# Matmuls of ones at the start, two earlier weight loads and a chunk-by-chunk second pair of tiles in a gated convolution and retention layer

## The chip, the cores and the metric

The kernel runs on one core of one Trainium2 chip. The metric is the device time in microseconds of one execution. The kernel before was timed three times, and its median is 1497.3 us.

## What is computed

One decoder layer over T = 1032 token columns, 1024 of a new sequence and 8 single tokens of other sequences. Cut to the part that the change touches, the reference is

```python
proj = rms_norm(x, n_mix_pre) @ w_in          # T x 1024 times 1024 x 7168
a_val, a_gate, q, k, v, g, gate_a, gate_b = split(proj)
u = a_val * sigmoid(a_gate)                   # T x 512, input of the 31-tap convolution
conv = depthwise_conv(concat(history, u)) + b_dw
```

Behind it come layer norm and SiLU of `conv`, the chunkwise retention of q, k and v, the gated merge with two output projections, and a squared-ReLU MLP of width 4096, with an RMS norm ahead of and behind both halves. Everything is 32-bit floating point.

## The kernel before, in words

Activations lie transposed: 128 channels on the partitions, T columns along them, and 8 such tiles `k` for the 1024 channels. The columns are cut in 3 chunks `c` of 344. Weights come in slots of four 128x128 tiles (256 KB), so that one output tile of 128 channels needs two slots, called its halves here (k 0 to 3 and k 4 to 7). Most products are made of three fast matmuls: an operand is split into a rounded high part (made by ScalarE, written ACT in the profile) and the rest as a low part, and high x high, high x low and low x high are summed in PSUM (`PARTS`, `tile_mms`, line 1026).

The kernel is raw: every engine has its own list of instructions in a fixed order, with semaphores between them. An instruction whose semaphore is not there blocks all behind it on its engine.

Output tiles are called groups g. Six PSUM banks form two sets of three, one bank for each chunk, and the groups take the sets in turn. The first groups make the four pairs (gate tile, value tile) of `u`:

- Pair 0 (`G_U`, `G_U + 1`) is made by `plain_mms` (line 1064) as full 32-bit matmuls from the raw `x_in` and weights `wp` with the norm gain multiplied in, before the norm of x is known. Slot `wp[:, 0]` is scaled by VectorE (DVE, line 2286), slots 1 to 3 by GpSimd (POOL, line 862). The order on TensorE (PE) is, for chunk 0: gate tile half 0 from `wp` 0, value tile half 0 from `wp` 1, gate half 1 from `wp` 2, value half 1 from `wp` 3. Chunks 1 and 2 go tile by tile. One column sum `x_stat` (line 1062) of each chunk feeds the root of the norm (`x_rms`, ACT lines 1527 and 1529), which writes `rr`. DVE then multiplies the six banks by `rr` (`u_factor`, line 2280), ACT makes the sigmoid of the gate tile (`u_gate(0)`, line 1576, which waits for five of the six `u_factor`), and DVE multiplies by it (`u_out(0)`, line 2355).
- Meanwhile `x_in` is normalised: `x_scale` (DVE 2264), `x_hi` (ACT 1557, high parts `xn_h`), `x_lo` (DVE 2272, low parts `xn_l`), each by chunk and half.
- Pair 1 (`G_U + 2`, `G_U + 3`) is made by `second_mms` (line 1078) from weight slots 4 to 7: first the gate tile over all three chunks, then the value tile over all three. A tile's two halves each raise the semaphore `mm` when they are done for the last chunk.
- Pairs 2 and 3 are made by `group8` (line 1031) from slots 8 to 15, one slot after the other, each over all three chunks.

The high parts of slots 8 and on are made on ACT by `weight_hi(n)` (line 1566); for n = 8 and 9 it waits until the slot n - 4 has been used for the last time, for those behind until the slot n - 2 has. On ACT it stands between other work:

```python
act.wait_ge(xn_lo, CHUNKS * KT)
for k in range(KT):
    x_gain(k)                 # L1580
    if k == 0:
        weight_hi(8)
    if k == 2:
        u_gate(1)
        weight_hi(9)
```

`u_gate(1)` waits until the gate tile of pair 1 is complete. The low parts are made on POOL by `low_part` (line 870). POOL makes the low part of slot 8, then waits for all eight `x_gain` (`pool.wait_ge(xs_sc, KT)`), then makes two sums `x_sum` (line 885), and then the low part of slot 9; from there one `x_sum` (lines 885 to 894) and one `low_part` take turns.

Of the kernel before, what the change touches and what calls it, by code (L numbers as in the profile page):

```python
# [24 lines left out]
ALU = mybir.AluOpType  # L25
ACT = mybir.ActivationFunctionType

P = 128
# [3 lines left out]
T = SEQ + DEC  # L32
CHUNKS = 3
# [5 lines left out]
HIST = TAPS - 1  # L39
# [34 lines left out]
G_U, S_U = 1, 0  # L74
# [40 lines left out]
LN_ADD, LN_SQUARE = {13: 1, 15: 2, 17: 3}, {10: (0, 1), 14: (2,), 16: (3,)}  # L115
ORDER = (0, 1, 3, 2, 5, 4, 6)
NSLOT = 264


def build(nc, xT, wseq, vecs, wdwT, cacheT, s_in, rope, mask_d, ident_d,  # L120
# [8 lines left out]
    with ExitStack() as ctx:  # L129
# [19 lines left out]
        u_ext, a_C1 = place("u_ext", [P, CT, UW])  # L149
        q0s, _ = place("q0s", [P, 2, T], F32, a_C1 + 4 * 2128)  # L150
# [4 lines left out]
        raw, _ = place("raw", [P, RAW, SLOT])  # L155
        w_h, _ = place("w_h", [P, HL, SLOT], F32R)
        w_l, _ = place("w_l", [P, HL, SLOT], F32R)
# [3 lines left out]
        sx_h, _ = place("sx_h", [P, 3, QK, HT], F32R, a_B)  # L161
        sx_l2, _ = place("sx_l2", [P, QK, HT], F32R, a_B + 12 * QK * HT)
        sx_l, _ = place("sx_l", [P, 2, QK, HT], F32R, a_A)
        sx_5, _ = place("sx_5", [P, QK, HT], F32, a_G + 4 * QK * HT)
        wx_h, _ = place("wx_h", [P, SLOT], F32R, a_C0)
        wx_l, _ = place("wx_l", [P, SLOT], F32R, a_C0 + 4 * SLOT)
        wx_x, _ = place("wx_x", [P, SLOT], F32, a_C0 + 8 * SLOT)
        wx_y, _ = place("wx_y", [P, SLOT], F32, a_C0 + 12 * SLOT)
        gst, _ = place("gst", [P, 8, HT], F32, a_G)
        gst_c, _ = place("gst_c", [P, 8, HT], F32, a_C1)  # L170
        sgm, _ = place("sgm", [P, 8, HT], F32, a_Y)
        silu, _ = place("silu", [P, T], F32, a_Q)
        cvq_h, _ = place("cvq_h", [P, T], F32R, a_Q)
        cva_h, _ = place("cva_h", [P, CT, T], F32R, a_B)
        cva_l, _ = place("cva_l", [P, CT, T], F32R, a_A)
        gt0, _ = place("gt0", [P, 4, T], F32, a_D)
        gt1, _ = place("gt1", [P, 4, T], F32, a_B + 16 * T)
        gb, _ = place("gb", [P, KT, T], F32, a_D)
        bop_b, _ = place("bop_b", [P, 4, T], F32, a_B)
        bop_a, _ = place("bop_a", [P, 2, T], F32, a_A + 8 * T)  # L180
        ma, _ = place("ma", [P, KT, T], F32, a_E)

        mg_h, _ = place("mg_h", [P, KT, T], F32R, a_A)
        mg_l, _ = place("mg_l", [P, KT, T], F32R, a_B)
        fx_h, _ = place("fx_h", [P, KT, T], F32R, a_A)
        fx_l, _ = place("fx_l", [P, KT, T], F32R, a_B)

        stg_a, _ = place("stg_a", [P, KT, T], F32, a_A)
        stg_b, _ = place("stg_b", [P, KT, T], F32, a_B)

        wp, _ = place("wp", [P, RAW, SLOT], F32, a_C2)
        wc_h, _ = place("wc_h", [P, 2, SLOT], F32R, a_C2 + 8 * T)
        wc_l, _ = place("wc_l", [P, 2, SLOT], F32R, a_C2 + 8 * T + 8 * SLOT)
        rr, _ = place("rr", [P, T], F32, a_G + 4 * T)
        cv_l, _ = place("cv_l", [P, CT, T], F32R, a_C2)
        qk1, _ = place("qk1", [P, 4, T], F32, a_C2)
        v1, _ = place("v1", [P, 4, T], F32, a_C1)
        ro1_h, _ = place("ro1_h", [P, 4, T], F32R, a_C2)
        ro1_l, _ = place("ro1_l", [P, 4, T], F32R, a_C1)
        h_res, _ = place("h_res", [P, KT, T], F32, a_C1)  # L200
        fac, _ = place("fac", [P, KT, T], F32, a_C0)
        op0, _ = place("op0", [P, QK, HT], F32, a_C0)
        hq_c, _ = place("hq_c", [P, 4, HT], F32, a_C0 + 8 * T)
        hq_d, _ = place("hq_d", [P, 8, HT], F32, a_C0 + 16 * T)
        hq_e, _ = place("hq_e", [P, 4, HT], F32, a_C0 + 32 * T)

        qk0, _ = place("qk0", [P, 4, T], F32, a_G)
        v0, _ = place("v0", [P, 4, T], F32, a_Y)
        ro0_h, _ = place("ro0_h", [P, 4, T], F32R, a_G)
        ro0_l, _ = place("ro0_l", [P, 4, T], F32R, a_Y)  # L210
        mix, _ = place("mix", [P, KT, T], F32, a_D)
        tx_l, _ = place("tx_l", [P, KT, T], F32R, a_D)

        wo_h, _ = place("wo_h", [P, 8, SLOT], F32R, a_E)
        wo_l, _ = place("wo_l", [P, 8, SLOT], F32R, a_E + 32 * SLOT)
        tx_h, _ = place("tx_h", [P, KT, T], F32R, a_E)

        sgt, _ = place("sgt", [P, T], F32, a_G)
        hist, _ = place("hist", [P, CT, DEC, TAPS], F32, a_Q)
        hprod, _ = place("hprod", [P, DEC, TAPS], F32, a_Q + 4 * CT * DEC * TAPS)  # L220
        hq_g, _ = place("hq_g", [P, 8, HT], F32, a_G)

        mask, _ = place("mask", [P, RC])
# [32 lines left out]
        def pset(g, n=CH):  # L256

            return ps[:, 3 * (g % 2):3 * (g % 2) + 3, 0:n]
# [4 lines left out]
        def t3(ap):  # L263

            return ap.rearrange("p (c n) -> p c n", c=CHUNKS)
# [142 lines left out]
        def done(slot):  # L408

            return slot + 1 + HL  # L410
# [163 lines left out]
        def taken(e, g, shift=0):  # L574


            e.wait_ge(ps_free[g % 2], shift + (g // 2 + 1))

        def free_set(pe, g, shift=0):

            if g >= 2:
                taken(pe, g - 2, shift)
# [15 lines left out]

        @block.sync
        def _(sp):  # L600
            sp.dma_start(x_in[:, 0:2, 0:CH], xT[:, 0:2, 0:CH]).then_inc(xa_in[0], 16)
            sp.dma_start(wp[:, 0, :], wseq[0]).then_inc(gate_ld[0], 16)
            sp.dma_start(x_in[:, 4:6, 0:CH], xT[:, 4:6, 0:CH]).then_inc(xa_in[2], 16)
            for s, n in ((1, 2), (2, 1), (3, 3)):
                sp.dma_start(wp[:, s, :], wseq[n]).then_inc(gate_ld[s], 16)
            for i in range(2):
                sp.dma_start(x_in[:, 4 * i:4 * i + 4, CH:2 * CH], xT[:, 4 * i:4 * i + 4, CH:2 * CH]
# [407 lines left out]
        def _(pe):  # L1015
# [48 lines left out]
            def plain_mms(c, t, half):  # L1064

                if c == 0 and half + t:
                    pe.wait_ge(w_split, 2 * half + t + 1)
                for sub in range(SLOT_TILES):
                    k = SLOT_TILES * half + sub
                    if (c, t) == (0, 0) and k in (0, 2):  # L1070
                        pe.wait_ge(w0_sc, k // 2 + 1)
                    if c == 0 and k % 2 == 0:
                        pe.wait_ge(xa_in[k // 2], 16)
                    out = pe.matmul(pch(G_U + t, c), wp[:, 2 * half + t, sub * P:(sub + 1) * P],  # L1074
                                    x_in[:, k, c * CH:(c + 1) * CH], start=(k == 0), stop=(k == KT - 1))
                return out

            def second_mms(t, c, half):
# [10 lines left out]
                                   (wc_h, wc_l) if t else W)  # L1089
                return out  # L1090

            plain_mms(0, 0, 0)
            plain_mms(0, 1, 0)
            plain_mms(0, 0, 1).then_inc(u_mm, 1)
# [13 lines left out]
            plain_mms(2, 1, 0)  # L1108
            plain_mms(2, 1, 1).then_inc(u_mm, 1)
            pe.sem_inc(mm, RAW)  # L1110
            for t in range(2):
                free_set(pe, G_U + 2 + t)
                for c in range(CHUNKS):
                    for half in range(2):
                        out = second_mms(t, c, half)
                        if c == CHUNKS - 1:
                            out.then_inc(mm, 1)
# [1102 lines left out]
        def _(dve):  # L2220
# [37 lines left out]
            def x_scale(c, half):  # L2258

                xs = x_in[:, 4 * half:4 * half + 4, c * CH:(c + 1) * CH]  # L2260
                if half == 0:
                    dve.wait_ge(rms_rs, R_X + c + 1)
                    dve.wait_ge(u_mm, 2 * c + 2)
                dve.tensor_tensor(xs, xs, rr[:, c * CH:(c + 1) * CH].unsqueeze(1).broadcast_to([P, 4, CH]), ALU.mult
                                  ).then_inc(x_sc, 1)
# [9 lines left out]
            def u_factor(c, t):  # L2275

                dve.wait_ge(rms_rs, R_X + c + 1)
                dve.wait_ge(u_mm, 2 * c + t + 1)
                rows = pch(G_U + t, c)
                dve.tensor_tensor(rows, rows, rr[:, c * CH:(c + 1) * CH], ALU.mult).then_inc(u_rr, 1)  # L2280

            dve.wait_ge(cst_ld, 16)
            dve.wait_ge(gate_ld[0], 16)
            for k in (0, 2):
# [12 lines left out]
            x_scale(1, 0)  # L2297
            u_factor(1, 0)
            u_factor(1, 1)
            x_scale(1, 1)  # L2300
            u_factor(2, 0)
            x_lo(1, 0)
            x_scale(2, 0)
            x_lo(1, 1)
            x_scale(2, 1)
            x_lo(2, 0)
            u_factor(2, 1)
            x_lo(2, 1)


# [34 lines left out]
            dve.wait_ge(wdw_ld, 48)  # L2345
            dve.wait_ge(hist_ld, 16)

            def u_out(j):

                g = G_U + 1 + 2 * j  # L2350
                if j == 0:
                    dve.wait_ge(u_rr, 2 * CHUNKS)
                dve.wait_ge(mm, done(S_U + 4 * j + 3))
                taken(dve, g - 1)
                dve.tensor_tensor(t3(u_ext[:, j, HIST:HIST + T]), pset(g), t3(sgt[:]), ALU.mult
                                  ).then_inc(ps_free[g % 2], 1)
                taken(dve, g)

            def u_sample(j):

                dve.tensor_copy(hist[:, j, :, HIST], u_ext[:, j, HIST + SEQ:HIST + T]).then_inc(h_done, 1)
# [17 lines left out]
                dve.tensor_tensor(sx_l2[:] if i == 2 else sx_l[:, i - 3], src, sx_h[:, i - 2].bitcast(F32),  # L2379
                                  ALU.subtract).then_inc(xs_lo, 1)  # L2380

            u_out(0)
            u_sample(0)
            taps(10)
            u_out(1)
# [768 lines left out]
```

## Time and profile before

| | |
|---|---|
| median of 3 runs | 1497.3 us |
| the 3 runs | 1497.29, 1497.96, 1497.30 us |
| span of the profiled execution | 1495.6 us |
| the profiled execution's own time | not recorded; the median is 1.7 us above the span |
| PE matmul busy | 1475.2 us, 99% |
| PE weight load busy | 1455.2 us, 97% |
| DVE, ACT, POOL busy | 1001.0, 635.4, 842.0 us |

The span runs from the first to the last instruction of the execution that the profiler took. Times in rows are microseconds from its start. "PE" is the matmul part of TensorE, "PEld" its weight loads. In a timeline a row is a run of like instructions: start, length, engine, line, operation, tiles, shape, count, and in brackets the idle time of the engine just ahead and what ended it. A 32-bit matmul shows as two records, the split kind as one.

### The profile page before, as it was taken

Reading aid. Unit: us, or ns where it says so; the run is one execution under the profiler, and the core shown is the slowest. Engines: PE = TensorE matmul, PEld = TensorE weight load, DVE = VectorE, ACT = ScalarE, POOL = GpSimd, SP = SyncE. Lnnn points to the kernel's source line nnn. Section 1 sums busy time; section 2 is a strip of 40 time slices with the busy share of each in tenths; the row PEclk is TensorE's granted clock in tenths of the full one; section 3 lists DMA queues with packets and bytes.
Section 4 is the critical chain, followed back from the end, with each engine's and each line's share of the span. In section 5 each row is a group of like instructions: output and inputs, shape, how many; then the busy total and the mean of one; then the engine's idle time right before and its main releaser. Section 6 shows DMA issues by size and latency. Waiting matters only on the chain.

```text
span 1495.6 us, 28307 instructions
## 1 busy us (share of the span) xinstructions
PE 1475.2 (99%) x11336; PEld 1455.2 (97%) x11336; DVE 1001.0 (67%) x1251; ACT 635.4 (42%) x929; POOL 842.0 (56%) x571
## 2 busy tenths in 40 slices
PE   8999999999999999999999999999999999999996
PEld 5999999999999999999999999999999999999995
DVE  7999888856545724576715876766657765574847
ACT  5533444344544541131213855556556332332333
POOL 3377776777545653257565445555555655554555
PEclk9999999999999999999999999999999999999998
DMA  6013333322356258621421144566759575454634
GB/s 217 22 42 94 114 114 113 113 80 65 112 176 205 75 200 296 219 80 50 149 78 50 29 149 171 199 237 219 253 193 326 203 285 189 142 208 156 227 107 170
DMA packets 110091, 229.13 MB, mean 153 GB/s; under 512 B 8960, under 2 KB 20992, under 8 KB 108304
## 3 DMA queue, kind: packets, MB, share of 16 engines
q1 hardware_dynamic: 95296, 204.30, 39.7%
q10 hardware_dynamic: 14672, 23.09, 4.6%
q8 instruction: 89, 1.46, 0.4%
q14 instruction: 34, 0.28, 0.1%
HBM read 154.41 MB, written 72.95 MB: 152 GB/s over the span
## 4 chain that ended last, share of the span: by engine, by line
PE 96%; POOL 1%; DMA 1%; ACT 1%; issue 1%; DVE 0%; POOLq 0%; SPq 0%; DVEq 0%; ACTq 0%
PE ps L1476 40%; PE ps L1237 26%; PE ps L1026 16%; PE ps L1402 3%; PE ps L1389 3%; PE ps L1074 2%; PE ps L1164 1%; PE ps L1169 1%; PE ps L1180 1%; PE ps L1166 1%; DMA cva_h<-conv_scratch 1%; PE ps L1147 0%; PE ps L1152 0%; PE ps L1194 0%; POOL w_l L931 0%
## 5 line engine op out<-in xcount | busy, mean ns | idle before, releaser
L1476 PE MATMUL ps<-tx_h,w_h 128*128 128x258 f32 x960 | 271.5, 283 | 0.0
L1476 PE MATMUL ps<-tx_l,w_h 128*128 128x258 f32 x960 | 271.3, 283 | 0.0
L1476 PE MATMUL ps<-tx_h,w_l 128*128 128x258 f32 x960 | 271.1, 282 | 0.0
L996 POOL TENSOR_TENSOR w_l<-raw,w_h 128x512 fp32r<-128x512 f32 x120 | 185.6, 1551 | 147.6 <-ACT w_h L2033 147.1
L1476 PE MATMUL ps<-fx_l,w_h 128*128 128x258 f32 x720 | 203.7, 283 | 0.0
L1476 PE MATMUL ps<-fx_h,w_h 128*128 128x258 f32 x720 | 203.6, 283 | 0.0
L1476 PE MATMUL ps<-fx_h,w_l 128*128 128x258 f32 x720 | 203.4, 282 | 0.0
L1476 PEld LDWEIGHTS ps<-tx_h,w_h 128*128 128x128 f32 x960 | 181.4, 189 | 0.1
L1476 PEld LDWEIGHTS ps<-tx_l,w_h 128*128 128x128 f32 x960 | 181.4, 189 | 0.1
L1476 PEld LDWEIGHTS ps<-tx_h,w_l 128*128 128x128 f32 x960 | 181.2, 189 | 0.0
L2328 DVE SCALAR_TENSOR_TENSOR ps<-u_ext,wdw,ps 128x512 f32<-128x512 f32 x232 | 155.2, 749 | 0.0
L2033 ACT ACTIVATE w_h<-raw 128x512 fp32r<-128x512 f32 x120 | 75.7, 631 | 186.8 <-PE ps L1476 179.7
L996 POOL TENSOR_TENSOR w_l<-sum_y,w_h 128x512 fp32r<-128x512 f32 x60 | 91.9, 1532 | 110.2 <-ACT w_h L2033 110.2
L1476 PEld LDWEIGHTS ps<-fx_h,w_h 128*128 128x128 f32 x720 | 136.2, 189 | 0.0
L1476 PEld LDWEIGHTS ps<-fx_l,w_h 128*128 128x128 f32 x720 | 136.0, 189 | 0.0
L1476 PEld LDWEIGHTS ps<-fx_h,w_l 128*128 128x128 f32 x720 | 135.9, 189 | 0.0
L1237 PE MATMUL ps<-xn_h,w_h 128*128 128x258 f32 x416 | 119.6, 287 | 0.0
L1237 PE MATMUL ps<-xn_l,w_h 128*128 128x258 f32 x416 | 117.5, 282 | 0.0
L1237 PE MATMUL ps<-xn_h,w_l 128*128 128x258 f32 x416 | 117.4, 282 | 0.0
L2884 DVE TENSOR_TENSOR fac<-ps,fac 128x516 f32<-128x516 f32 x79 | 54.6, 691 | 83.3 <-PE ps L1476 83.3
L931 POOL TENSOR_TENSOR w_l<-raw,w_h 128x512 fp32r<-128x512 f32 x54 | 76.6, 1418 | 55.2 <-ACT w_h L1650 55.1
L850 POOL TENSOR_TENSOR w_h<-raw,zero 128x512 fp32r<-128x512 f32 x36 | 42.0, 1167 | 108.8 <-PE ps L1026 50.2
(386 smaller groups left out, 4305.4 us busy)
## 6 DMA issues: line engine op xcount, KB each, us to landing
raw<-wseq_dram SPq DMA_DIRECT2D x260, 256.0 KB, 3.1
quad_scratch<-quad_h SPq DMA_DIRECT2D x16, 774.0 KB, 3.5
tx_h<-quad_scratch SPq DMA_DIRECT2D x12, 1032.0 KB, 10.4
tx_l<-hidden_scratch SPq DMA_DIRECT2D x12, 1032.0 KB, 12.8
gate_scratch<-gst SPq DMA_DIRECT2D x10, 1032.0 KB, 5.0
hidden_scratch<-hq_g SPq DMA_DIRECT2D x8, 1032.0 KB, 7.0
hidden_scratch<-stg_b SPq DMA_DIRECT2D x6, 1032.0 KB, 6.9
hq_g<-hidden_scratch SPq DMA_DIRECT2D x6, 1032.0 KB, 13.1
```

Source lines behind the costliest of these rows:

```text
L850: pool.tensor_tensor(hi, raw[:, s, :], zero[:, 0:1].broadcast_to([P, SLOT]), ALU.add).then_inc(w_hi, 1)
L931: pool.tensor_tensor(lo, src, hi.bitcast(F32), ALU.subtract).then_inc(xw_lo, 1)
L996: pool.tensor_tensor(lo, src, hi.bitcast(F32), ALU.subtract).then_inc(q_lo, 1)
L1026: out = pe.matmul(pch(g, c), w[a][:, place_, sub * P:(sub + 1) * P], xs[b][:, k, c * CH:(c + 1) * CH], start=(first and n == 0), stop=(las ...
L1074: out = pe.matmul(pch(G_U + t, c), wp[:, 2 * half + t, sub * P:(sub + 1) * P], x_in[:, k, c * CH:(c + 1) * CH], start=(k == 0), stop=(k == ...
L1237: out = pe.matmul(ps[:, 2 * n + s, 0:HC], XRINGS[q % RING][wa][:, kk * P:(kk + 1) * P], x_operand(i, xb, kk, s), start=(i < 3 and kk == 0 ...
L1389: out = pe.matmul(pch(g, m), (wo_h, wo_l)[a][:, slot, sub * P:(sub + 1) * P], MG[b][:, k, c * CH:(c + 1) * CH], start=(k == 0 and n == 0), ...
L1402: out = pe.matmul(pch(g, c), DIRECT_W[slot][a][:, (k % SLOT_TILES) * P:(k % SLOT_TILES + 1) * P], FX[b][:, k, c * CH:(c + 1) * CH], start= ...
L1476: out = pe.matmul(ps[:, 2 * n + s, 0:HC], RINGS[q % RING][wa][:, kk * P:(kk + 1) * P], OPS[x][xb][:, QK * kh + kk, at_:at_ + HC], start=(i ...
L2033: act.activation(RINGS[q % RING][0], src, ACT.Copy).then_inc(q_hi, 1)
L2328: out = dve.scalar_tensor_tensor(dst, u_, w_, bank, ALU.mult, ALU.add)
L2884: dve.tensor_tensor(dst, pair(n), dst, ALU.add).then_inc(ev_d, 1)
```

## The change

Four things are changed:

- Ahead of the first product PE issues nine matmuls of a 128x128 tile of ones by itself into PSUM bank 6, whose content is not used.
- On the queue of SyncE (SP) the load of `wp` 0 goes ahead of that of the first two tiles of x, and the load of `wp` 1 goes ahead of x tiles 4 and 5 instead of behind them.
- Pair 1 goes chunk by chunk: for each chunk first the gate tile and then the value tile.
- On DVE `u_factor(2, 0)` goes ahead of `x_scale(1, 1)`, and `u_factor(2, 1)` and `u_out(0)` go behind it, ahead of `x_lo(1, 0)`. `u_out(0)` stood behind the last `x_lo` before.

The lists of ACT and POOL are the same.

```diff
+WARM = 9
...
         def _(sp):
+            sp.dma_start(wp[:, 0, :], wseq[0]).then_inc(gate_ld[0], 16)
             sp.dma_start(x_in[:, 0:2, 0:CH], xT[:, 0:2, 0:CH]).then_inc(xa_in[0], 16)
-            sp.dma_start(wp[:, 0, :], wseq[0]).then_inc(gate_ld[0], 16)
+            sp.dma_start(wp[:, 1, :], wseq[2]).then_inc(gate_ld[1], 16)
             sp.dma_start(x_in[:, 4:6, 0:CH], xT[:, 4:6, 0:CH]).then_inc(xa_in[2], 16)
-            for s, n in ((1, 2), (2, 1), (3, 3)):
+            for s, n in ((2, 1), (3, 3)):
...
+            for _ in range(WARM):
+                pe.matmul(B6[:, 0:P], ones[:], ones[:], start=True, stop=True)
             plain_mms(0, 0, 0)
...
-            for t in range(2):
-                free_set(pe, G_U + 2 + t)
-                for c in range(CHUNKS):
+            for c in range(CHUNKS):
+                for t in range(2):
+                    if c == 0:
+                        free_set(pe, G_U + 2 + t)
                     for half in range(2):
                         out = second_mms(t, c, half)
                         if c == CHUNKS - 1:
...
             u_factor(1, 0)
             u_factor(1, 1)
+            u_factor(2, 0)
             x_scale(1, 1)
-            u_factor(2, 0)
+            u_factor(2, 1)
+            u_out(0)
             x_lo(1, 0)
             x_scale(2, 0)
             x_lo(1, 1)
             x_scale(2, 1)
             x_lo(2, 0)
-            u_factor(2, 1)
             x_lo(2, 1)
...
-            u_out(0)
             u_sample(0)
             taps(10)
```

## Rows read from the trace of the kernel before

**Rows 1.** The page: busy time of each engine over the span.
```profile
PE 1475.2 (99%) x11336; PEld 1455.2 (97%) x11336; DVE 1001.0 (67%) x1251; ACT 635.4 (42%) x929; POOL 842.0 (56%) x571
```

**Rows 2.** Waits of PE over the whole span (total, times, longest).
```profile
PE ps L1074 <- DVE wp L2286: 5.8, 1, 5.8
PE ps L1237 <- ACT v L1853: 0.2, 1, 0.2
```

**Rows 3.** Timeline of PE.
```profile
5.78 12.39 PE L1074 MATMUL ps<-x_in,wp 128*128 128x344 f32 x32 [5.78 <-DVE wp L2286]
...
31.31 7.10 PE L1074 MATMUL ps<-x_in,wp 128*128 128x344 f32 x24
38.21 0.42 PE L1026 MATMUL ps<-xn_h,w_h 128*128 128x344 f32 x1
...
66.64 0.64 PE L1026 MATMUL ps<-xn_h,w_h 128*128 128x344 f32 x3
```

**Rows 4.** Timeline of the weight loads, 3 to 19 us.
```profile
11.07 0.34 PEld L1074 LDWEIGHTS ps<-x_in,wp 128*128 128x128 f32 x1 [0.24 <-issue]
11.65 5.98 PEld L1074 LDWEIGHTS ps<-x_in,wp 128*128 128x128 f32 x21 [0.24 <-issue]
```

**Rows 5.** Windows: stretch, length, busy time by engine, PEclk (granted clock), DMA share, GB/s.
```profile
6.00:8.00 2.00, 2.00 (x4) 1.26 (x5) 0.89 (x2) 1.14 (x2) 0.00 (x0) 1.00 1.08 388
...
1486.00:1488.00 2.00, 0.00 (x0) 0.00 (x0) 2.00 (x5) 0.00 (x0) 2.00 (x2) 0.55 0.82 309
```

**Rows 6.** Timeline of PE: 128-column matmuls of retention, and the last matmuls.
```profile
383.15 1.05 PE L1164 MATMUL ps<-p_b,vt_b 128*128 128x128 f32 x8
...
1478.63 2.78 PE L1498 MATMUL ps<-hq_g,ones 128*128 128x258 f32 x12
```

**Rows 7.** Timeline of DVE, 16 to 50 us.
```profile
19.90 5.13 DVE L2264 TENSOR_TENSOR x_in<-x_in,rr 128x1376 f32<-128x1376 f32 x2
...
32.73 1.58 DVE L2264 TENSOR_TENSOR x_in<-x_in,rr 128x1376 f32<-128x1376 f32 x1
34.23 0.94 DVE L2280 TENSOR_TENSOR ps<-ps,rr 128x344 f32<-128x344 f32 x2
35.07 1.58 DVE L2264 TENSOR_TENSOR x_in<-x_in,rr 128x1376 f32<-128x1376 f32 x1
36.57 0.52 DVE L2280 TENSOR_TENSOR ps<-ps,rr 128x344 f32<-128x344 f32 x1
37.00 2.03 DVE L2272 SCALAR_TENSOR_TENSOR xn_l<-x_in,vec,xn_h 128x344 fp32r<-128x344 f32 x4
...
48.23 1.23 DVE L2355 TENSOR_TENSOR u_ext<-ps,sgt 128x1032 f32<-128x1032 f32 x1
```

**Rows 8.** Timeline of ACT, 31 to 70 us.
```profile
34.34 2.00 ACT L1557 ACTIVATE xn_h<-x_in,vec 128x344 fp32r<-128x344 f32 x4 [0.52 <-DVE x_in L2264]
37.13 1.03 ACT L1576 ACTIVATE sgt<-ps 128x1032 f32<-128x1032 f32 x1 [0.78 <-DVE ps L2280]
...
48.35 1.16 ACT L1580 ACTIVATE x_in<-x_in,vec 128x1032 f32<-128x1032 f32 x1 [2.32 <-DVE xn_l L2272]
49.41 0.61 ACT L1566 ACTIVATE w_h<-raw 128x512 fp32r<-128x512 f32 x1
...
53.46 5.33 ACT L1580 ACTIVATE x_in<-x_in,vec 128x1032 f32<-128x1032 f32 x5
66.90 0.63 ACT L1566 ACTIVATE w_h<-raw 128x512 fp32r<-128x512 f32 x1 [8.11 <-PE ps L1026]
```

**Rows 9.** Timeline of POOL.
```profile
8.63 4.30 POOL L862 TENSOR_TENSOR wp<-wp,vec 128x512 f32<-128x512 f32 x3 [7.80 <-DMA wp<-wseq_dram]
...
58.87 4.77 POOL L885 TENSOR_TENSOR sx<-x_in 128x1032 f32<-128x1032 f32 x2 [7.47 <-ACT x_in L1580]
63.60 1.29 POOL L870 TENSOR_TENSOR w_l<-raw,w_h 128x512 fp32r<-128x512 f32 x1
```

More of the change, by code:

```diff
@@ L2280, in u_factor, with u_out @@
                 dve.tensor_tensor(rows, rows, rr[:, c * CH:(c + 1) * CH], ALU.mult).then_inc(u_rr, 1)
+            def u_out(j):
+                g = G_U + 1 + 2 * j
+                if j == 0:
+                    dve.wait_ge(u_rr, 2 * CHUNKS)
+                dve.wait_ge(mm, done(S_U + 4 * j + 3))
+                taken(dve, g - 1)
+                dve.tensor_tensor(t3(u_ext[:, j, HIST:HIST + T]), pset(g), t3(sgt[:]), ALU.mult
+                                  ).then_inc(ps_free[g % 2], 1)
+                taken(dve, g)
             dve.wait_ge(cst_ld, 16)
@@ L2346, in _ @@
             dve.wait_ge(hist_ld, 16)
[L2348 to L2357, printed above, removed]
             def u_sample(j):
```

## The prediction

> **What bounds the kernel now.** I read the page's busy times first, then the waits of PE, then the timelines of the four engines over the first 110 us, because all edits lie there. PE is busy 99% of the span [rows 1]. It waits 5.8 us for its first operands and otherwise never over 0.2 us [rows 2]. So PE is the bound from 5.78 us on: what an edit does to its time is what it adds or takes in the instants at which PE may go on, and any new idle time of PE, wherever it lies, ends up in the total almost whole. Whoever reads this should look for two numbers: when the split products start (38.21 us, [rows 3]) and when the second slot of the third pair, slot 9, starts (66.64 us, [rows 3]).
>
> The first part runs slowly. A weight load followed the last every 0.57 us or so up to 11.65 us (11.07 to 11.65), then 21 in 5.98 us, 0.285 each [rows 4]. That is a factor of two, the ratio of the two levels of TensorE's clock, 1.2 and 2.4 GHz. The granted clock reads 1.00 there all the same [rows 5]; the pace is the better witness. About 5.9 us of PE's time were at the low level, so a warm start would shorten PE's own list by up to 2.9 us.
>
> **The change, part by part.**
>
> *Nine matmuls of ones.* Eight records of 128 columns took 1.05 us warm, which holds a drain, so some 0.11 to 0.13 us each [rows 6]; nine 32-bit matmuls are 18 records, at half pace some 4.0 to 4.7 us. Starting at about 1 us, they end between 5 and 5.8, in time that is idle now. I take nothing for them. If they started late they could hold up the first product by up to 1 us; the next paragraphs show that PE has that much room.
>
> *Loads.* `wp` 0 goes out one issue (0.5 us) sooner and `wp` 1 jumps over one load. The first scaling on POOL starts at 8.63 us, and three take 4.30 us [rows 9]; it may start 0.5 to 0.9 us sooner. The four eight-record pieces of chunk 0 take 2.29 us each at full pace. With PE at full pace from about 5.3 us, the first ends at 7.6 us and PE then waits for `wp` 1, scaled at about 9.3 us. Chunk 0 ends at 9.3 + 3 x 2.29 = 16.2 us instead of 18.0, and the whole plain part, whose end by its last row is 31.31 + 7.10 = 38.4 us with its drain [rows 3], some 1.8 us sooner: the next product could start at 36.4 us. So of 2.9 us of clock some 1.1 go to the wait for `wp` 1.
>
> *What that is worth.* The split products need the PSUM set that `u_gate(0)` frees. It ran from 37.13 to 38.16, having waited for `u_factor(2, 0)` (36.57 to 37.09), and PE went on at 38.21 [rows 3, 7, 8]. DVE works without a gap from 19.90 to there [rows 7]; it is held by its own list and by data from memory, not by PE. So PE's gain stops at this gate. The gate moves by the other edit: `u_factor(2, 0)` now starts at about 35.1 and ends at 35.65, and `u_gate(0)` can go as soon as ACT ends `x_hi(1, 0)`, which is held by DVE's `x_scale(1, 0)` and ends at 36.34 [rows 8]. It then runs from 36.25 to 37.3, and the split products start at 37.35: **0.86 us gained**, bounds 0 (a gate as late as before) and 1.8 (PE's own pace).
>
> Here a rule weighs against the row. The Trainium skill (TensorE: Matmul & The Clock Gate, "The HAM clock gate") says that the throttled clock is the default and that activity releases it, so that early matmuls run at half rate. By that alone the ones would bring the whole 2.9 us. The rows agree on the pace and deny the worth, since the engine behind is the one that frees the banks.
>
> *DVE's new order.* Between `x_scale(1, 1)` and `x_lo(1, 0)` now come 0.43 us of `u_factor(2, 1)` and 1.23 us of `u_out(0)`, so that the last `x_lo` ends at about 49.8 instead of 48.3 us [rows 7]. PE reads chunk 1 from 44.9 and chunk 2 from 52.4 us in the new order (24 matmuls of 0.158 us for each tile and chunk: 28.43 us for 180 of them, [rows 3]), and no low part is late. `u_out(0)` ends at 38.9, well ahead of 41.1 us, when the value tile wants its set. Nothing lost, nothing gained here; a wait is bounded by 0 on both sides.
>
> *Chunk by chunk.* This part hurts. Before, the gate tile of pair 1 was finished after 72 matmuls, about 49.6 us. Now it is finished after 120, and its first half after 108. ACT does `x_gain(0)` and then `weight_hi(8)`, which waits for that first half. Before there was no wait: it ran at 49.41 [rows 8]. Now it can run at 37.35 + 107 x 0.158 + 0.32 + 0.11 = 54.7 us (0.32 the length of the last matmul, 0.11 from its end to ACT, as at 66.90, [rows 8]). Behind it in ACT's list are seven `x_gain`, `u_gate(1)` and `weight_hi(9)`, which took from 49.41 to 58.79 = 9.38 us [rows 8]; `u_gate(1)` itself has no further wait (56.2 against 57.3). So the last `x_gain` ends at 64.1 us, 5.3 later. POOL waits for all eight before its two sums: 58.87 becomes 64.15. The low part of slot 9, 63.60 + 1.29 = 64.89 before, follows 6.0 us behind their start [rows 9], so it is there at **70.15 us**. PE wants it after 180 matmuls, at 37.35 + 28.4 = 65.8 us. It had 1.7 us to spare and now waits 4.4 us. Slot 9 starts at 70.2 instead of 66.64: **+3.55 us**, the 0.86 included.
>
> In one line: slot 9's start less before = (split start) + 32.85 - 66.64. Start 37.35 gives +3.55; 36.4 gives +2.6; 38.2 gives +4.4.
>
> *Behind that.* Does it get worse, or is it caught up? POOL goes on with a sum (2.4 us) and slot 10's low part at about 73.6, wanted at 75.9; slot 11 about 79.8, wanted at 81.5; then each slot's high part waits for PE itself again, as before. DVE is 0.3 us late only and starts to wait for PE at its third `u_out`. So everything locks on to PE, 3.55 us late, and since PE has no idle time left to the end, nothing is returned. Sum against the profiled span: 1495.6 + 3.55 = 1499.15; the median stands 1.7 us above that span, so 1500.9 us.
>
> **The rivals.**
>
> *The clock falls in the wait.* After the last matmuls (end 1481.4, [rows 6]) the clock is at 1.00 until just past 1486 and then at half (0.55 over 1486 to 1488, [rows 5]): some 4.8 us of idleness. The new wait is 4.4 us, close to that. If it falls near the wait's end, PE goes at half pace for up to the 5.9 us that the first rise took, and loses up to 2.9 us: 1500.9 to 1503.8, say 1503. Against it: 4.4 is below 4.8, and the only case seen is one. The same page of the Trainium skill says that the gate's point of switching depends on where the activity falls against a free-running counter, so the same program may fall in one run and not in another. Chance 0.18.
>
> *PE's pace carries the head.* If DVE and ACT also come sooner (less waiting for the first sums), the split products start at 36.4 and the loss is +2.6 us, 1499.9. Against: DVE has no gap between 19.90 and 37 [rows 7]. With it go smaller stalls than I count. Chance 0.14.
>
> *The late slot is hidden.* The change is not slower if slot 9's low part is there when PE comes, so that the 0.86 us are kept: 1496.4 us. The place is POOL's wait for the eight `x_gain`. It decides where that end passes 64.1 - 4.4 = 59.7 us, 0.9 us later than before. It would need ACT to reach `weight_hi(8)` by 50.3 us, when the gate tile's last chunk has not begun. Chance 0.04.
>
> *The whole of the cold start comes back.* PE's 2.9 us, with no gate at 37.3, no wait for `wp` 1 and no late slot: 1494.4 us. Three of the steps above would have to be wrong together. Chance 0.01. The skill's rule on the gate, taken alone, gives this.
>
> *The edits at the head do nothing.* Start 38.2, +4.4 us, 1501.7: part of my own range.
>
> **How the numbers follow.** My case (+2.8 to +4.4) has 0.63, the fallen clock 0.18, the faster head 0.14, the hidden slot and the whole cold start 0.05 together. The range runs from 1499.4 to 1503.8: it holds my case, the clock and most of the faster head. A difference of 0.2% is 3.0 us, about what a measurement can tell from none. Slower by over that: the clock and most of my case, 0.74; within: the faster head and the lower edge of my case, 0.22; faster by over it would need 3 us where the gate allows 1.8 at most, 0.04.
>
> **What would show it.** In the profile after: plain weight loads at 0.285 us before 8 us; `u_factor(2, 0)` ahead of 36 us; the split products from about 37.3; ACT idle some 3.5 us ahead of `weight_hi(8)` at 54.7; POOL's two sums from 64.1; one PE wait of about 4.4 us for POOL's low part (line 870), ending at 70.2, and hardly any other but that for `wp` 1. I am wrong if no such wait is there, or if PE waits again at slots 10 or 11, or if the matmuls behind the wait run at half pace.

## The result and the profile after

The changed kernel takes 1502.98 us (median of 5 runs, 1502.14 to 1503.62) against 1497.32 us before (5 runs). The ratio is 1.0037, with a 95% interval of [1.0026, 1.0047]: 5.7 us slower. The forecast was 1500.9 us in a range of 1499.4 to 1503.8, with 1503 as the time of the rival in which the clock falls. The profiled execution is the 1502.98 us one, its span 1500.9 us (most line numbers are higher by 2 to 6 than before). Of all runs told of below one, of the kernel without ones, fell in a slow state of the chip (2419.41 us at a mean granted clock of 0.556) and is left out of the figures.

The page's busy row and PE's waits, which answer to [rows 1, 2]:

```profile
PE 1479.5 (99%) x11354; PEld 1459.9 (97%) x11354; DVE 1001.9 (67%) x1251; ACT 635.5 (42%) x929; POOL 843.0 (56%) x571
```
```profile
PE ps L1028 <- POOL w_l L872: 4.4, 1, 4.4
PE ps L1028 <- ACT sgt L1581: 1.1, 1, 1.1
PE ps L1095 <- DVE eps_b L2236: 1.1, 1, 1.1
```

One new wait for POOL's low part (line 872) stands out, 4.4 us. A second, 1.1 us for the first sigmoid, is the measure of how far PE now runs ahead of that gate. PE's timeline (start, length, line, tiles, count), for [rows 3]:

```profile
5.41 10.40 PE L1076 MATMUL ps<-x_in,wp 128*128 128x344 f32 x32
...
28.94 7.10 PE L1076 MATMUL ps<-x_in,wp 128*128 128x344 f32 x24
37.16 0.43 PE L1028 MATMUL ps<-xn_h,w_h 128*128 128x344 f32 x1 [1.12 <-ACT sgt L1581]
...
65.14 0.62 PE L1028 MATMUL ps<-xn_h,w_l 128*128 128x344 f32 x3
70.13 1.23 PE L1028 MATMUL ps<-xn_h,w_h 128*128 128x344 f32 x3 [4.37 <-POOL w_l L872]
71.16 1.06 PE L1028 MATMUL ps<-xn_l,w_h 128*128 128x344 f32 x3
...
74.60 0.76 PE L1028 MATMUL ps<-xn_h,w_l 128*128 128x344 f32 x3
75.20 0.62 PE L1028 MATMUL ps<-xn_h,w_h 128*128 128x344 f32 x3
```

Slot 9 starts at 70.13, 3.49 us later than before. Behind it PE goes at little over half its pace until 75.20. The windows of that stretch (PE busy and count first, granted clock third from the end) say why:

```profile
66.00:68.00 2.00, 0.00 (x0) 0.00 (x0) 1.97 (x2) 0.49 (x1) 2.00 (x2) 1.00 0.00 0
68.00:70.00 2.00, 0.00 (x0) 0.00 (x0) 1.93 (x3) 0.00 (x0) 2.00 (x2) 0.51 0.00 0
70.00:72.00 2.00, 1.87 (x6) 1.87 (x7) 2.00 (x5) 0.00 (x0) 2.00 (x2) 0.50 0.37 114
72.00:74.00 2.00, 2.00 (x8) 2.00 (x8) 2.00 (x5) 0.00 (x0) 2.00 (x3) 0.50 0.08 26
74.00:76.00 2.00, 2.00 (x12) 2.00 (x12) 2.00 (x5) 0.00 (x0) 2.00 (x1) 0.79 0.43 131
```

The clock fell to half about 68 us, some 2.3 us into the wait, and came back near 74.8. From 71.16 to 74.60 there are four steps from trio to trio (a trio is one row of three matmuls, one for each chunk), 0.86 us each, where full pace has 0.47. Of the 4.7 us that PE worked at half pace, 4.7 x (1 - 0.47 / 0.86) = 2.1 us are lost. With the 3.49 us of lateness that makes 5.6; the measured difference is 5.7 between the medians and 5.3 between the two profiled spans.

The chain that makes slot 9 late, in the timelines of ACT, POOL and DVE ([rows 7 to 9]):

```profile
36.10 1.01 ACT L1581 ACTIVATE sgt<-ps 128x1032 f32<-128x1032 f32 x1
...
49.60 1.16 ACT L1585 ACTIVATE x_in<-x_in,vec 128x1032 f32<-128x1032 f32 x1 [1.90 <-DVE xn_l L2277]
54.50 0.63 ACT L1571 ACTIVATE w_h<-raw 128x512 fp32r<-128x512 f32 x1 [3.75 <-PE ps L1028]
...
58.56 5.33 ACT L1585 ACTIVATE x_in<-x_in,vec 128x1032 f32<-128x1032 f32 x5
```
```profile
63.97 4.71 POOL L887 TENSOR_TENSOR sx<-x_in 128x1032 f32<-128x1032 f32 x2 [7.46 <-ACT x_in L1585]
68.65 1.43 POOL L872 TENSOR_TENSOR w_l<-raw,w_h 128x512 fp32r<-128x512 f32 x1
```
```profile
34.08 1.36 DVE L2285 TENSOR_TENSOR ps<-ps,rr 128x344 f32<-128x344 f32 x3
35.35 1.58 DVE L2269 TENSOR_TENSOR x_in<-x_in,rr 128x1376 f32<-128x1376 f32 x1
```

ACT stands for 3.75 us ahead of slot 8's high part, which now waits for PE; everything behind it on ACT's list, the last five `x_gain` included, is that much later; POOL's two sums start at 63.97 instead of 58.87; slot 9's low part comes at 70.08.

### The profile page after: what moved, and what is told of

The parts are those of the page before. It is cut to its first block, busy times and chain, and to the rows that moved or that the text cites. A ratio compares the mean times of both kernels' runs of the same rounds, so it can differ in the third digit from the quotient of the medians.

```text
span 1500.9 us, 28344 instructions
## 1 busy us (share of the span) xinstructions
PE 1479.5 (99%) x11354; PEld 1459.9 (97%) x11354; DVE 1001.9 (67%) x1251; ACT 635.5 (42%) x929; POOL 843.0 (56%) x571
## 4 chain that ended last, share of the span: by engine, by line
PE 94%; POOL 2%; DVE 2%; ACT 1%; issue 1%; DMA 1%; SPq 0%; POOLq 0%; DVEq 0%; ACTq 0%
PE ps L1481 40%; PE ps L1242 26%; PE ps L1028 15%; PE ps L1407 3%; PE ps L1394 3%; PE ps L1169 1%; PE ps L1174 1%; PE ps L1185 1%; PE ps L1171 1%; DMA x_in<-xT_dram 1%; PE ps L1152 0%; PE ps L1157 0%; PE ps L1199 0%; DVE x_in L2269 0%; ACT x_in L1585 0%
## 5 line engine op out<-in xcount | busy, mean ns | idle before, releaser
L933 POOL TENSOR_TENSOR w_l<-raw,w_h 128x512 fp32r<-128x512 f32 x54 | 76.7, 1421 | 54.7 <-ACT w_h L1655 54.6
```

What stands on the lines that cost most here:

```text
L933: pool.tensor_tensor(lo, src, hi.bitcast(F32), ALU.subtract).then_inc(xw_lo, 1)
```

## The experiments

All run beside the kernel before; its median was 1497.66 us for the first four, 1497.62 for the next four and 1497.48 for the last. Theory at the start: the late slot 9 costs 3.5 us, and the clock that falls in its wait costs 2 more.

### The low part of slot 9 ahead of the sums

```diff
                 low_part(n % RAW, n)
-                if n == 2 * RAW:
+                if n == 2 * RAW + 1:
                     pool.wait_ge(xs_sc, KT)
                     x_sum(0)
-                if 2 * RAW <= n < 15:
+                    x_sum(1)
+                if 2 * RAW < n < 15:
                     x_sum(n - 2 * RAW + 1)
```

> The changed kernel with one move on GpSimd: the low part of slot 9 goes ahead of the wait for the eight x_gain and of the two sums, which then stand behind it with the third. My theory (the late slot 9 costs 3.5 us and the clock that falls in its 4.4 us of waiting some 2 more): slot 9's low part is there at about 60 us, PE does not wait for it and the clock stays up. Left are small waits because the sums still start at 64.0: slot 10 at 72.4 instead of 71.3 (1.1 us), slot 11 some 0.5 more; split products from 37.2. So 1497.3 - 1.05 + 1.6 = 1497.9 us. Rival (the loss lies in pair 1 going chunk by chunk, or in VectorE's new order, by contention or late banks, and the wait for slot 9 is only where it shows): the time stays over 1500.

Measured: 1497.59 us, ratio 1.0000 [0.9991, 1.001] to the kernel before. POOL's timeline and PE's waits:

```profile
58.62 1.29 POOL L872 TENSOR_TENSOR w_l<-raw,w_h 128x512 fp32r<-128x512 f32 x1 [2.23 <-ACT w_h L1572]
```
```profile
PE ps L1029 <- POOL w_l L872: 1.4, 2, 1.1
```

Slot 9's low part is there at 59.9 us, PE's 4.4 us wait is gone, 1.1 us is left for slot 10, and the clock reads 1.00 in every window from 66 to 78. Moving one operation on an engine that the change did not touch takes back the whole loss: the split products start at 37.06, 1.15 us sooner than before, and the small waits for low parts (1.4 us together) take that up. So going chunk by chunk has no further cost that shows here.

### The wait filled with matmuls of ones

```diff
+            def filler(k):
+                if k == SLOT_TILES - 1:
+                    free_set(pe, G_U + 5)
+                    for _ in range(16):
+                        pe.matmul(pch(G_U + 5, 0)[:, 0:P], ones[:], ones[:], start=True, stop=True)
...
+            group8(G_U + 4, S_U + 8, XN, 0, 0, filler)
```

> The changed kernel with 16 matmuls of the tile of ones between slot 8 and slot 9, into a bank that is free and is overwritten later (the loop of the last two pairs is written out for it). They take some 3.7 us of the 4.4 us wait, and the slot arrives as late as before. My theory: PE goes on at 70.1 us as in the changed kernel, but at full pace, so that only the late slot is paid: 1497.3 + 3.5 = 1500.8 us, granted clock 1.00 from 66 to 76 us. Rival (what is lost behind 70 us is not the clock but late weights or contention of the engines): 1503.0 as the changed kernel, or more.

Measured: 1500.79 us, ratio 1.0021 [1.0011, 1.0031]. PE's timeline and the windows:

```profile
65.36 3.73 PE L1128 MATMUL ps<-ones 128*128 128x128 f32 x32
69.91 0.75 PE L1029 MATMUL ps<-xn_h,w_h 128*128 128x344 f32 x3 [0.82 <-POOL w_l L873]
70.49 0.63 PE L1029 MATMUL ps<-xn_l,w_h 128*128 128x344 f32 x3
```
```profile
68.00:70.00 2.00, 1.18 (x11) 0.99 (x10) 1.93 (x4) 0.00 (x0) 2.00 (x3) 1.00 0.00 0
70.00:72.00 2.00, 2.00 (x13) 2.00 (x14) 2.00 (x4) 0.00 (x0) 2.00 (x1) 1.00 0.33 121
```

Slot 9 is as late as in the changed kernel (69.91), but PE goes on at full pace. 1502.98 - 1500.79 = 2.2 us is the clock's part, 1500.79 - 1497.66 = 3.1 us that of the lateness. This splits the loss. The changed kernel was timed at another time, beside a kernel before of 1497.32 and not 1497.66; with each taken against its own, the clock's part is 2.5 us.

### No matmuls of ones

> The changed kernel without the nine matmuls of ones. My theory (the split products wait for the sigmoid of the first gate tile, whose chain does not hang on PE's pace): the plain weight loads go at 0.57 us until 8 to 12 us, the plain products end up to 1.5 us later, which the 1.1 us wait for the sigmoid mostly takes in: the same as the changed kernel within 0.4 us, 1503.0. Rival (the cold clock costs what PE's list says): 1.5 to 2.9 us slower, 1504.5 to 1505.9.

Its edit takes the two lines of the loop over `WARM` out. Measured: 1502.57 us (1502.37 to 1503.05), ratio 1.0033 [1.0019, 1.0046]: no slower than the changed kernel. The weight loads, and the first split product:

```profile
8.16 0.34 PEld L1076 LDWEIGHTS ps<-x_in,wp 128*128 128x128 f32 x1 [0.24 <-issue]
8.73 7.57 PEld L1076 LDWEIGHTS ps<-x_in,wp 128*128 128x128 f32 x26 [0.24 <-issue]
```
```profile
37.39 0.42 PE L1028 MATMUL ps<-xn_h,w_h 128*128 128x344 f32 x1 [0.30 <-ACT sgt L1579]
```

The loads are at half pace until 8.73 us; the split products still wait for the sigmoid, 0.3 us instead of 1.1, and start at 37.39. That is 0.23 us later than with the ones, since the gate takes in nearly all that they save. The wait for slot 9 is again 4.4 us and the clock falls here too, but it stays down for 3.4 us only (70.5 to 73.9) and not for 6.8; that makes up for the 0.23. So the ones bring nothing in the changed kernel.

### Pair 1 tile by tile again

> The changed kernel with PE's order of pair 1 put back, tile by tile. My theory: ACT's high part of slot 8 runs at 50.7 without a wait and the last x_gain ends at 60.1, so that slot 9 comes at 66.2, before PE wants it; instead PE waits 1.5 us in chunk 2 for low parts that VectorE's new order makes later. Slot 9 starts at about 67.0 against 66.6 before: 1497.7 us. Rival (chunk by chunk is not what makes slot 9 late, the later low parts of x are): a wait of over 3 us for slot 9 stays, 1500.5 or more.

Its edit puts PE's two loops back as they were. Measured: 1497.88 us, ratio 1.0002 [0.9993, 1.0012]. PE's longest wait and ACT's last gains:

```profile
PE ps L1028 <- ACT xn_h L1561: 1.3, 1, 1.3
```
```profile
54.56 5.34 ACT L1584 ACTIVATE x_in<-x_in,vec 128x1032 f32<-128x1032 f32 x5
```

The gains end at 59.9 as expected, slot 9 is on time, and PE waits 1.3 us once in chunk 2 for the later parts of x (the wait is put down to `xn_h`, made from 45.55 us on; the low part is made from 45.44 on). So it is PE's order that makes slot 9 late, and DVE's order without it costs back the 1 us that it gains. The chunk-by-chunk order is what DVE's order needs, and ACT's and POOL's lists are what it needs in turn.

### Half the wait

The edit leaves one sum ahead of slot 9's low part, and puts the second behind it with the third.

> The changed kernel with one sum on GpSimd, not two, ahead of the low part of slot 9 (the second goes behind it, with the third). It halves the wait: slot 9 comes at about 67.7 us, PE waits 2.1 us there, some 0.4 us for slot 10 (the third sum is now ahead of it) and up to 0.6 us for slot 11. My theory (the clock falls because the one wait is 4.4 us long): the granted clock stays at 1.00 and only the waits are paid, 1.5 to 2.1 us above the kernel before: about 1499.4 us. Rival (any wait of some us in this place brings the clock down): 2 us more, 1501.4, with half clock in the windows from 66 to 76 us.

Measured: 1501.93 us, ratio 1.003 [1.0018, 1.0042], in two groups: the profiled run took 1499.3, five others 1501.7 to 1502.4. The profiled one:

```profile
67.46 0.75 PE L1030 MATMUL ps<-xn_h,w_h 128*128 128x344 f32 x3 [1.89 <-POOL w_l L872]
```
```profile
68.00:70.00 2.00, 2.00 (x11) 2.00 (x10) 1.96 (x3) 0.00 (x0) 2.00 (x2) 0.65 0.43 139
70.00:72.00 2.00, 2.00 (x9) 2.00 (x8) 2.00 (x4) 0.00 (x0) 2.00 (x1) 0.50 0.00 0
```

Against the theory the clock fell here too, behind a wait of 1.9 us. I took the upper group to be runs in which it stayed down for longer, and tried that with the next two.

### Half the wait, filled, and half the wait once more

> The half-wait kernel with eight matmuls of the tile of ones (1.8 us) in its 1.9 us wait, ahead of slot 9. The half-wait kernel was 1501.9 us, 2.5 above what its waits explain, so my first theory on when the clock falls (the one wait must be near 4.8 us long) is wrong. New theory: an idle time of 1.9 us brings the clock down for part of the runs or nearly all of them, and its price is higher than in the changed kernel, since more work runs at half pace: with the wait filled, only lateness is paid, slot 9 0.8 us later than before, slots 10 and 11 up to 0.4 and 0.6: 1498.5 to 1499.4 us in every run. Rival (the 1501.9 comes from slots 10 and 11, or from another state of the chip): 1501.5 or more.

Measured: 1501.63 us (1501.2 to 1504.77), ratio 1.0034 [1.002, 1.0047]: the rival. The granted clock is 1.00 in every window from 60 to 120 us, and the kernel is slower than the profiled run in which the clock fell. PE's timeline, then POOL's and DVE's:

```profile
104.60 0.75 PE L1031 MATMUL ps<-xn_h,w_h 128*128 128x344 f32 x3 [1.12 <-POOL w_l L873]
```
```profile
88.39 3.42 POOL L873 TENSOR_TENSOR w_l<-raw,w_h 128x512 fp32r<-128x512 f32 x1 [2.56 <-ACT w_h L1581]
...
101.31 3.24 POOL L873 TENSOR_TENSOR w_l<-raw,w_h 128x512 fp32r<-128x512 f32 x1 [1.75 <-ACT w_h L1581]
```
```profile
88.36 2.30 DVE L2395 TENSOR_TENSOR sx_l<-x_in,sx_h 128x2064 fp32r<-128x2064 f32 x1
...
101.12 2.30 DVE L2395 TENSOR_TENSOR sx_l<-x_in,sx_h 128x2064 fp32r<-128x2064 f32 x1
```

> The half-wait kernel once more, for a look. Of its six runs one took 1499.3 us, and that was the profiled one, with half clock from 68.5 to 71.9 us; five took 1501.7 to 1502.4. Theory: the upper group has half clock for twice as long, some 6.8 us behind the wait, which costs 3.4 us. Rival: the upper group shows the same fall and one more wait.

The half-wait kernel once more took 1499.17 us and had the fallen clock again, so no profile shows a run of the upper group. What is known of that group is its mean granted clock: 0.996 to 0.997 in the five runs of 1501.7 to 1502.4, against 0.995 in both of 1499.2 to 1499.3. As far as means that differ by 0.001 can tell, the upper group is that in which the clock did not fall, and its spans (1499.9 to 1500.4) lie within those of the filled kernel (1499.2 to 1502.7). In the once-more run, POOL's low part of the same slot:

```profile
88.47 1.29 POOL L872 TENSOR_TENSOR w_l<-raw,w_h 128x512 fp32r<-128x512 f32 x1 [2.56 <-ACT w_h L1573]
```

Here the chain of sums and low parts on POOL has no slack left and runs beside PE to the end of the pair. With PE at full pace, DVE's low-part operation starts in the same instant as POOL's (88.36 and 88.39), and POOL's takes 3.42 us instead of 1.29; the same happens at 101.3. PE waits at both places, 0.36 and 1.12 us, and 0.32 and 0.21 us at slots 10 and 11. Its first matmul behind the four pairs starts at 110.39 us, against 108.85 in the half-wait kernel's first profile, where the clock fell and none of these waits is there. In that profile the value tile of a pair is done about half a microsecond later (DVE's `u_out` starts at 86.31, not 85.85), and DVE's operation starts at 89.58, when POOL's low part is through. The two engines meet there as well, but on a sum that holds nobody up:

```profile
89.58 2.30 DVE L2387 TENSOR_TENSOR sx_l<-x_in,sx_h 128x2064 fp32r<-128x2064 f32 x1
```
```profile
89.59 4.57 POOL L896 TENSOR_TENSOR x_in<-x_in 128x1032 f32<-128x1032 f32 x1
```

So a fallen clock that makes a kernel faster by some 2.5 us is no contradiction: it moved two engines out of each other's way where PE would have waited. That POOL is slow when it meets this operation of DVE also shows in the kernel before, where PE does not wait for it:

```profile
101.65 3.52 POOL L931 TENSOR_TENSOR w_l<-raw,w_h 128x512 fp32r<-128x512 f32 x1 [2.07 <-ACT w_h L1650]
```
```profile
101.73 2.29 DVE L2379 TENSOR_TENSOR sx_l<-x_in,sx_h 128x2064 fp32r<-128x2064 f32 x1
```

The slow-down is thus seen in several traces; that it is what parts the two groups is read from them and was not tried by itself.

### ACT's and POOL's lists fitted to the new order

```diff
                 x_gain(k)
-                if k == 0:
+                if k == 3:
                     weight_hi(8)
-                if k == 2:
+                if k == 5:
                     u_gate(1)
                     weight_hi(9)
```

together with the first experiment's edit.

> The changed kernel with the low part of slot 9 ahead of the sums on GpSimd, as in the first experiment, and with ACT's list fitted to the new order: four x_gain ahead of the high part of slot 8, two more ahead of u_gate(1) and the high part of slot 9, the last two behind. The x_gain then end at 60.6 instead of 64.0 us, slots 10 and 11 are ready at 69.1 and 75.4, wanted at 71.3 and 77.0. My theory: no wait of PE after the start of the split products at 37.2, so the gain of 1.0 us at the sigmoid is kept: 1.0 us faster than the kernel before, about 1496.5. Rival (the chunk-by-chunk order has costs of its own): no faster than the kernel before.

Measured: 1496.01 us, ratio 0.9989 [0.998, 0.9998], 1.6 us faster than the kernel before. PE's waits:

```profile
PE ps L1029 <- ACT sgt L1582: 1.4, 1, 1.4
PE ps L1096 <- DVE eps_b L2237: 1.1, 1, 1.1
```

No wait for a low part of a weight over 0.2 us is left, and the gain at the sigmoid is kept. It was taken too low: the split products started at 36.97, 1.24 us sooner than before. Another 0.4 us shows in the medians, whose cause stays open.

### The sigmoid ahead of x_hi

```diff
-            x_hi(1, 0)
             u_gate(0)
+            x_hi(1, 0)
             x_hi(1, 1)
```

on top of the last.

> As the kernel with both lists fitted, and ACT makes the sigmoid of the first gate tile ahead of x_hi(1, 0), which held it until 36.1 us. It then starts at 35.5 when the fifth u_factor is there, and the split products start at 36.5 instead of 37.2; VectorE's low parts come as before, since they are behind u_out(0) on its list. My theory: 0.6 us less again, 1.7 us faster than the kernel before, about 1495.8. Rival (VectorE's low parts or GpSimd's sums are next in line): no change against the kernel with both lists fitted.

Measured: 1495.37 us (1495.05 to 1495.85), ratio 0.9985 [0.9976, 0.9994], 2.25 us faster than the kernel before and the fastest of the study.

```profile
35.45 1.03 ACT L1582 ACTIVATE sgt<-ps 128x1032 f32<-128x1032 f32 x1 [3.93 <-DVE ps L2286]
```
```profile
36.53 0.42 PE L1029 MATMUL ps<-xn_h,w_h 128*128 128x344 f32 x1 [0.42 <-ACT sgt L1582]
```

The sigmoid starts at 35.45 and the split products at 36.53, as expected. PE now waits only 0.4 us for the gate, so its own pace at the head is nearly the bound.

### The same without the ones

> The fastest kernel so far (both lists fitted, sigmoid first) without the nine matmuls of ones. There the split products start at 36.5, 0.4 us after PE is free, so PE's own pace at the head is nearly the bound. Theory: the ones are worth something here, where they were worth nothing in the changed kernel: the plain products end between 37.1 and 38.3 us, by the instant at which the clock rises: 0.6 to 1.8 us slower, 1496.0 to 1497.2, with more spread. Rival: no change, 1495.4.

Measured: 1496.56 us (1495.75 to 1497.52), ratio 0.9994 [0.9985, 1.0003]. Its weight loads:

```profile
10.82 0.34 PEld L1077 LDWEIGHTS ps<-x_in,wp 128*128 128x128 f32 x1 [0.24 <-issue]
11.38 5.97 PEld L1077 LDWEIGHTS ps<-x_in,wp 128*128 128x128 f32 x21 [0.23 <-issue]
```

The pace doubles at 11.4 us here, no wait for the sigmoid is left, and the split products start at 37.72, 1.19 us later than with the ones. (The profiled run, 1497.22 us, is one of the slower ones.) The ones are worth 1.2 us in this kernel, and nothing in the changed one.

### The first two edits alone

> The kernel before with the first two edits alone: nine matmuls of ones, and the two weight loads sooner; orders of PE and VectorE as before. My theory (the split products wait for the sigmoid that hangs on VectorE's list): PE's plain products end up to 1.8 us sooner and PE then waits about 1 us for the sigmoid; the split products start at 38.0 to 38.2: 0 to 0.2 us faster than the kernel before. Rival (the first part's clock is on the path): 1.0 to 1.8 us faster.

Measured: 1497.41 us, ratio 1.0002 [0.9993, 1.0011], in two groups: six runs of 1497.0 to 1497.4 and five of 1498.5 to 1498.9. PE's wait at the sigmoid:

```profile
37.83 0.42 PE L1028 MATMUL ps<-xn_h,w_h 128*128 128x344 f32 x1 [2.28 <-ACT sgt L1580]
```

The head's gain is swallowed by the gate, as said. The mean granted clock of the six lower runs is 0.996 to 0.997, of the five upper ones 0.995.

> The kernel with the first two edits alone, and nine more matmuls of ones (2.0 us) in PE's 2.3 us wait for the sigmoid ahead of the split products. Without them its runs lay in two groups, six at 1497.0 to 1497.4 and five at 1498.5 to 1498.9. Theory: the upper group are runs in which the clock fell in or behind the 2.3 us wait; with the wait filled all runs lie at 1497.0 to 1497.4. Rival (the two groups have another cause, such as the clock's state at the start): two groups as before.

Measured with the wait filled: 1497.22 us, ratio 1.0 [0.9991, 1.0009]. Eight of eleven runs lie at 1496.9 to 1497.3, and three at 1498.3 to 1498.9; none has a mean clock under 0.996. This fits the theory that the clock falls in or behind the 2.3 us wait in about half of the runs, costs some 1.5 us then, and stays up when the wait is filled. It is shown by the mean clocks and the times only: the profiled run of the unfilled kernel is one of the lower group, with the clock at 1.00 from 30 to 42 us. The three higher runs of the filled kernel have another cause, which stays open (two of them have a span of 1495.5 to 1495.6, near the others, and more time around it).

## Why the prediction was right, and where it was not

- **The gate at the head.** Forecast: `u_gate(0)` from 36.25, split products at 37.35, PE's plain end at 36.4. Measured: 36.10, 37.16 and 28.94 + 7.10 = 36.04. DVE's `u_factor(2, 0)` came where it was put. Ahead of the gate two terms were off without any worth: the weight loads were at full pace from 6.6 us and not from 5.3, and `wp` 1 was ready for its first weight load at 8.60 us (0.61 us of wait there) and not at 9.3, since POOL began to scale it at 6.77 and not at about 7.9. That PE's faster head is worth nothing beyond the gate was shown by the kernel without ones (same time) and the one with the head alone (ratio 1.0002).
- **The clock rule set against the row.** By the rule of the Trainium skill (TensorE: Matmul & The Clock Gate, "The HAM clock gate") that early matmuls run at half rate, taken alone, the ones would have brought 2.9 us. Measured: nothing in the changed kernel, 1.2 us where the gate is out of the way. The wait for the gate decided.
- **The late slot.** Forecast: `weight_hi(8)` at 54.7, sums from 64.1, slot 9 at 70.15, a wait of 4.4 us, +3.55. Measured: 54.50, 63.97, 70.08, 4.37 and +3.49. Each step of the chain through ACT's and POOL's lists held within 0.2 us, and the first experiment removes the loss by one of its links.
- **Behind the wait.** Slots 10 and 11 were on time and everything locked on to PE, as forecast, in the changed kernel. It was closer than I wrote: in the half-wait kernel with the wait filled PE waited there, 0.32 and 0.21 us.
- **The step that failed: the clock.** The likeliest case took it to stay up, "4.4 is below 4.8", from the one fall at the end of the trace, and gave the fall 0.18. It fell, and with it came one of the prediction's own signs of being wrong, matmuls at half pace behind the wait. The mean granted clock was 0.995 in four of the five runs, against 0.996 to 0.997 for the kernel before; the fifth, at 0.996, took 1502.1 us, where lateness alone gives 1500.8, so that it fell there too is likely. The price came from the right row, up to 2.9 us; it is 2.2 to 2.5. One fall behind a long idle stretch shows that the clock can fall after 4.8 us of idleness, and nothing about shorter ones. The Trainium skill (TensorE: Matmul & The Clock Gate, "The HAM clock gate") says that the switching point varies with where the activity lies. The traces here agree: in a wait of the same 4.4 us the clock fell 2.3 us after PE's last matmul in the changed kernel, and 4.5 us after it in the one without ones. A case that rests on one instance should have left the rival far more than 0.18.
- **The sum.** 3.1 us of lateness and 2.2 to 2.5 of clock, by the filled wait. The likeliest case named 1500.9 us, which is what the kernel with the filled wait took, 1500.8; the rival named 1503, which is what the changed kernel took. The measured time lies outside the likeliest case (+2.8 to +4.4 us, 1500.1 to 1501.7) and inside the stated range only because the range had been drawn to take in that rival. So the size of the late slot was forecast, and that the total fell in the range was in part luck.

## What to carry to other kernels

When PE's order is changed, follow each engine's list behind every wait that is tied to the moved product: here one high part that waited 3.75 us on ACT held up eight unrelated operations, and through them a weight slot two engines away. Gains ahead of a gate are worth nothing until the gate moves; ask first what the next wait hangs on. Price a new wait of PE twice (here from 1.9 us on), once for its length and once for the clock that may fall in it, and where it can't be removed, fill it.

## What the runs showed of the hardware

- Behind a wait of 4.4 us the clock fell in two of two profiles, and nine of ten runs have a mean granted clock of 0.994 to 0.995 (the tenth 0.996). Behind 1.9 us it fell in two of seven runs, both profiled. Behind 2.3 us five of eleven runs have a mean of 0.995, none of them profiled. Behind waits of 1.0 to 1.4 us no profile shows a fall. In the 4.4 us wait it fell about 2.3 us after PE stopped in the changed kernel, and only about when PE went on in the one without ones; behind the 1.9 us wait it fell when PE had been going again for 1.1 and 0.8 us. It stayed down for 6.8 us in the changed kernel and for 3.4 us in the three other profiles that show it.
- The rise at the start moves too: the weight loads reach full pace at 8.73 us in one kernel without ones and at 11.38 in another, both having started between 5.5 and 5.7. With the ones from 1.07 us on it moves as well. In the changed kernel it came at about 6.6, so that the first three loads of the first product were still at half pace; in six other kernels with ones the loads are at full pace from their first, at 5.3 to 5.5, and in the kernel with the filled 4.4 us wait only from 7.2 on.

```profile
6.11 0.34 PEld L1076 LDWEIGHTS ps<-x_in,wp 128*128 128x128 f32 x1 [0.24 <-issue]
6.64 1.35 PEld L1076 LDWEIGHTS ps<-x_in,wp 128*128 128x128 f32 x5 [0.19 <-issue]
```

- A POOL operation on two tiles of 128x512 takes 1.29 us by itself and 3.2 to 3.6 us where it starts within 0.2 us of a DVE operation of 2064 columns (2.3 us); a POOL operation of 1032 columns takes 4.57 us there instead of 2.43. DVE's own operation keeps its 2.3 us in these meetings.
